# Six and ten recurrence steps in two halves' stretches instead of eight and eight, and the second attention over 66 products

## The reference, cut to what matters

```python
h = rmsnorm(x, g_pre[l]) * (1.0 + scale[:, None]) + shift[:, None]
p = h @ w_in[l]                       # (2048, 8704)
y_pool = pool_mixer(a_in, ...) * silu(a_g)
y_hgrn = hgrn2_mixer(b_q, b_f, b_i, ...) * silu(b_g)
y_conv = short_conv_mixer(c_x, c_b, c_c, conv_w[l]) * silu(c_g)
y_diff = diff_attention(d_q, d_k, d_v, ...) * silu(d_g)
# the recurrence, over chunks of tokens:
o = einsum(qc * exp(b), S) + einsum(scores, vc)
S = exp(b_last) * S + einsum(kc * exp(b_last - b), vc)
# the merge:
merged = sum(gates[n] * (y[n] @ w_merge[n]));  out = merged @ w_out[l]
x = x + gate * rmsnorm(out, g_post[l])
```

## The kernel before

| engine | offsets |
|---|---|
| SyncE | -15 `load_in3`, -13 `load_pool` (two loads, L599 and L600, counted by `a_loaded`), -1 `load_conv`, `load_gate`, +7, +13, +15 stores |
| ScalarE | -11 `pool_sigmoid` (L1078) and `sigmoids` (L1062 to L1064), -10 `affine`, -9 table preload and `logs`, -7 `key_decays`, -5 and -1 `level_decays` (L1095), 0 `query_decays` (L1101), +1 `gate_sigmoid`, `conv_sigmoid`, +5 `tokens`, +9 `squares`, +13 `root_h` (L1107, L1108) |
| VectorE | -10 `shares`, -9 `queries`, -8 `scan`, -7 to -2 differences (L1416, folded by L1421) and decays, +1, +3, +5, +7 `pick`, +11 `advance_state` (L1465, L1468), +12 `pool_out`, +14 `finish` |
| GpSimd | -4 `pool_part` (L822 to L835), 0 `decays_second`, +2 `conv_part` |
| TensorE | 0, 2, 4, 6 `rounds` (L1817), +4 `transposes`, +8 `outputs` (L1834 to L1841), +12 `norms` (L1847) |

## Time and profile before

### The profile page before, as it was taken

One profiled execution on the slowest core, in us unless ns is written; L12 is line 12 of the kernel. 1 busy time (PEld: TensorE's weight loads), 2 busy tenths in 40 slices (PEclk: granted clock), 3 DMA queues, 4 the chain that ended last, 5 costly groups with the idle time before them and its releaser, 6 DMA issues. The chain is left out here.

```text
span 2533.1 us, 35157 instructions
## 1 busy us (share of the span) xinstructions
PE 2274.4 (90%) x11572; PEld 1871.5 (74%) x11572; DVE 1434.6 (57%) x2638; ACT 1144.1 (45%) x2400; POOL 839.4 (33%) x739
## 2 busy tenths in 40 slices
PE   3698799998999889898999999999999966989898
PEld 2486677777777668687888888878888844767676
DVE  5676566655888777312766666445556334444442
ACT  3553455543544543422666666434434233434341
POOL 0113223223745645200222222124343225244353
PEclk7799999999999989999999999999999988999999
DMA  6799777757767667989464654588777676576581
GB/s 227 260 352 328 259 231 241 223 204 277 264 239 261 230 222 253 332 265 264 163 191 146 181 169 149 171 258 250 230 247 235 213 238 178 155 190 187 148 226 61
DMA packets 383963, 564.75 MB, mean 223 GB/s; under 512 B 32432, under 2 KB 248880, under 8 KB 382768
## 3 DMA queue, kind: packets, MB, share of 16 engines
q1 hardware_dynamic: 315248, 313.01, 42.0%
q10 hardware_dynamic: 68544, 249.59, 27.8%
HBM read 331.28 MB, written 231.21 MB: 222 GB/s over the span
## 5 line engine op out<-in xcount | busy, mean ns | idle before, releaser
L1682 PE MATMUL gb<-h_hi,w_both 128*128 128x512 f32 x1904 | 789.0, 414 | 87.2 <-ACT o L949 41.7
L1684 PE MATMUL gb<-h_hi,w_both 128*128 128x512 f32 x1904 | 757.7, 398 | 0.0
L1683 PE MATMUL gb<-h_lo,w_both 128*128 128x512 f32 x1904 | 756.7, 397 | 0.0
L1682 PEld LDWEIGHTS gb<-h_hi,w_both 128*128 128x128 f32 x1904 | 366.9, 193 | 171.2 <-issue 91.7
L1684 PEld LDWEIGHTS gb<-h_hi,w_both 128*128 128x128 f32 x1904 | 365.7, 192 | 81.2
L1683 PEld LDWEIGHTS gb<-h_lo,w_both 128*128 128x128 f32 x1904 | 367.7, 193 | 67.1
L949 ACT ACTIVATE o<-gb 128x512 f32<-128x512 f32 x272 | 161.4, 594 | 372.5 <-PE gb L1684 308.0
L809 POOL TENSOR_TENSOR C_prob<-C_prob,C_cf 128x512 f32<-128x512 f32 (+3 forms) x160 | 156.9, 1005 | 506.1 <-DVE C_cf L1358 492.1
L1014 ACT ACTIVATE C_prob<-C_sc,C_negm 128x512 f32<-128x512 f32 (+3 forms) x320 | 198.5, 622 | 246.6 <-DVE C_negm L1336 239.9
L1250 DVE TENSOR_TENSOR o<-gb,o 128x512 f32<-128x512 f32 x204 | 140.3, 688 | 231.0 <-PE gb L1684 220.0
L1240 DVE TENSOR_TENSOR w_both<-w,w_both 128x512 fp32r<-128x512 f32 x170 | 142.1, 836 | 171.5 <-ACT w_both L922 171.1
(11 more groups left out here) (230 smaller groups left out, 3722.6 us busy)
## 6 DMA issues: line engine op xcount, KB each, us to landing
wS_scratch<-w_both ACTq DMA_DIRECT2D x238, 512.0 KB, 4.4
w_both<-wS_scratch ACTq DMA_DIRECT2D x238, 512.0 KB, 4.3
w<-in_w_in_dram SPq DMA_DIRECT2D x68, 512.0 KB, 5.2
gT_scratch<-o SPq DMA_DIRECT2D x128, 256.0 KB, 4.6
D_gate<-gT_scratch SPq DMA_DIRECT2D x32, 1024.0 KB, 9.8
pT_scratch<-o SPq DMA_DIRECT2D x80, 256.0 KB, 4.2
C_qt<-qB_scratch SPq DMA_DIRECT2D x128, 128.0 KB, 3.4
C_ks<-kT_scratch SPq DMA_DIRECT2D x48, 256.0 KB, 5.7
```

Of the source, the lines that this page charges most:

```text
L1682: mm(to, hi[:, k, :], h_hi[j][:, k, :], start=(fresh and k == 0), stop=False, skip_group_check=True)
L1683: mm(to, hi[:, k, :], h_lo[j][:, k, :], start=False, stop=False, skip_group_check=True)
L1684: last = mm(to, lo[:, k, :], h_hi[j][:, k, :], start=False, stop=(k == KH - 1), skip_group_check=True)
```

## The change

It sets new bases: six steps in the first half's stretch, at slots 130, 146, ..., 210 (16 apart), and ten in the second's, at 367, 377, 388, 398, ..., 461 (10 and 11 in turn). Steps 6 and 7, which work on the first half's tokens, thereby run in the second half's stretch. `MIX_FROM` takes the place of `MIX_HALF` where the boundary between the stretches is meant; where the tokens' halves are meant, `MIX_HALF` stays. The second attention is spread over 66 slots, and the mixers after it start five slots earlier. eb and kt are doubled; their second copies lie in the last, unused level of QX and X. Their waits reach two steps back. `advance_state` moves from offset 11 to 10 and `pool_out` from 12 to 10.

```diff
-ATTENTION = ((50, 60), (284, 71))
-
-MIX_BASE = [130 + 12 * i for i in range(8)] + [372 + 25 * i // 2 for i in range(8)]
+ATTENTION = ((50, 60), (284, 66))
+
+MIX_BASE = [130 + 16 * i for i in range(6)] + [367 + 21 * i // 2 for i in range(10)]
+
+MIX_FROM = (0, 6, 16)
...
-            eb, qe, kt = sb("eb", [P, 2, P]), sb("qe", [P, 2, P]), sb("kt", [P, 2, P])
+            qe = sb("qe", [P, 2, P])
...
+            eb, kt = [sb("eb", [P, 2, P]), QX[:, :, NL - 1, :]], [sb("kt", [P, 2, P]), X[:, :, NL - 1, :]]
...
             def mixers_over(half):
-                n = MIX_HALF * (half + 1)
+                n = MIX_FROM[half + 1]
...
-                    if n == MIX_BASE[MIX_HALF * half] - 17:
+                    if n == MIX_BASE[MIX_FROM[half]] - 17:
                         begin_mixers(half)
...
             def key_decays(i):
                 act.wait_ge(scanned, i + 1)
-                if i:
-                    act.wait_ge(t_done, i)
+                if i >= 2:
+                    act.wait_ge(t_done, i - 1)
...
             def query_decays(i):
-                if i:
-                    act.wait_ge(state_done, i)
-                    act.wait_ge(qe_ready, i)
-                a(eb[:, :, :], b_s[:, :, :], ACT.Exp).then_inc(eb_ready, 1)
+                if i >= 2:
+                    act.wait_ge(state_done, i - 1)
+                    act.wait_ge(qe_ready, i - 1)
+                a(eb[i % 2][:, :, :], b_s[:, :, :], ACT.Exp).then_inc(eb_ready, 1)
...
-                i = mix_step(n, 11)
+                i = mix_step(n, 10)
                 if i is not None:
                     advance_state(i)
-                i = mix_step(n, 12)
+                i = mix_step(n, 10)
                 if i is not None:
                     pool_out(i)
...
                 if u >= NU:
-                    pe.wait_ge(fin_done, MIX_HALF)
-                    pe.wait_ge(yp_ready, MIX_HALF)
-                    pe.wait_ge(state_done, MIX_HALF)
+                    pe.wait_ge(fin_done, MIX_FROM[1])
+                    pe.wait_ge(yp_ready, MIX_FROM[1])
+                    pe.wait_ge(state_done, MIX_FROM[1])
...
-                if i % MIX_HALF == 0:
-                    pe.wait_ge(b_setup, i // MIX_HALF + 1)
-                    pe.wait_ge(b_consts, 16 * (9, 17)[i // MIX_HALF])
+                if i in MIX_FROM:
+                    pe.wait_ge(b_setup, MIX_FROM.index(i) + 1)
+                    pe.wait_ge(b_consts, 16 * (9, 17)[MIX_FROM.index(i)])
```

More of the change, by code:

```diff
@@ L714, in _ @@
                 for half in range(HALVES):
-                    if n == MIX_BASE[MIX_HALF * half] - 17:
+                    if n == MIX_BASE[MIX_FROM[half]] - 17:
                         begin_mixers(half)
-                    if n == MIX_BASE[MIX_HALF * half] - 16:
+                    if n == MIX_BASE[MIX_FROM[half]] - 16:
                         load_blocks(half)
@@ L1086, in key_decays @@
                 act.wait_ge(scanned, i + 1)
-                if i:
-                    act.wait_ge(t_done, i)
+                if i >= 2:
+                    act.wait_ge(t_done, i - 1)
                 for t in range(2):
-                    ins = a(kt[:, t, :], b_s[:, t, :], ACT.Exp, bias=b_s[:, t, P - 1:P], scale=-1.0)
+                    ins = a(kt[i % 2][:, t, :], b_s[:, t, :], ACT.Exp, bias=b_s[:, t, P - 1:P], scale=-1.0)
                 ins.then_inc(decayed, 1)
@@ L1424, in decay_keys @@
                 dve.wait_ge(decayed, i + 1)
-                tt(kt[:, :, :], kt[:, :, :], k_s[i % 2][:, :, :], ALU.mult).then_inc(kt_ready, 1)
+                tt(kt[i % 2][:, :, :], kt[i % 2][:, :, :], k_s[i % 2][:, :, :], ALU.mult).then_inc(kt_ready, 1)
             def decay_queries(i):
@@ L1430, in decay_queries @@
                     dve.wait_ge(o_done, i)
-                tt(qe[:, :, :], q_s[i % 2][:, :, :], eb[:, :, :], ALU.mult).then_inc(qe_ready, 1)
+                tt(qe[:, :, :], q_s[i % 2][:, :, :], eb[i % 2][:, :, :], ALU.mult).then_inc(qe_ready, 1)
             def decay_first_queries(i):
@@ L1467, in advance_state @@
                 for t in range(2):
-                    ins = stt(S[:, t, :], S[:, t, :], eb[:, t, P - 1:P], kvm[:, t, :], ALU.mult, ALU.add)
+                    ins = stt(S[:, t, :], S[:, t, :], eb[i % 2][:, t, P - 1:P], kvm[:, t, :], ALU.mult, ALU.add)
                 ins.then_inc(state_done, 1)
@@ L1855, in transposes @@
                     nc.tensor.transpose(b6[:, t, :], in3[i % 2][:, 4 + t, :], ident[:, :])
-                    last = nc.tensor.transpose(b6[:, 2 + t, :], kt[:, t, :], ident[:, :])
+                    last = nc.tensor.transpose(b6[:, 2 + t, :], kt[i % 2][:, t, :], ident[:, :])
                 last.then_inc(t_done, 1)
```

## The result

The changed kernel takes 2552.89 us (median of 7 runs, 2548.96 to 2562.11), the kernel before, on the same chip, 2536.46 us (7 runs). The ratio is 1.0081 with a 95% interval of 1.0067 to 1.0095: slower by 0.8%. Forecast were 2543 us and slower. The time lies in the range (2512 to 2567), 10 us above the forecast.

What follows compares the result with a forecast made beforehand. TensorE, busy 90% of the span, was taken as the bound. 2534.9 - 39.3 (first stretch) + 0 (attention) + 50.0 (last stretch) = 2545.6 us profiled, less 3.0 for the median: 2543 us, range 2512 to 2567.

Steps and rivals of the forecast that it cites:

- What bounds it; the prices: Whole kernel: TensorE, busy 90% of the span, is the bound; a product costs 2.72 us, a recurrence step 8.45 us.
- First stretch, -39.3 us beside the moved work: Products 130 to 229: ScalarE's queue falls apart with steps 16 apart, so 49.3 us of loss shrink to 10.
- the rest: Products 130 to 229: loss left by VectorE's full slots, 10 us for six steps, half clock included, bounds 3 and 31.
- the forecast's own test: Stated sign of being wrong: TensorE without gaps at 1.00 in the last stretch, or over 20 us lost in the first.
- Second attention, 0: Products from 284, 66 instead of 71: TensorE is the bound and released products cost the same later; 0, bounds -3 and +4.
- Last stretch, 50 us of loss: Products 367 to 475: eight late pool loads stall ScalarE, then TensorE; 33.2 us idling plus 16.8 of lower clock.
- the loop that I worked out: Last stretch: outputs free win, GpSimd's pool work, then SyncE's load; 9.6 us against 3.3 available, ScalarE standing 6.3 us.
- Lifted waits: Last stretch: doubled eb and kt lift waits at no instruction cost; the earlier state update keeps ahead of the next outputs.
- The sum: Whole kernel: 2534.9 - 39.3 + 0 + 50.0 = 2545.6 us profiled, 3.0 less for the median, say 2543 us.
- Rival 1: Last stretch: quick 2.4 us landings mostly hide the new wait, stalls too short for the clock; 2505 us, chance 0.13.
- Rival 2: Last stretch: 7.5 us landings lengthen the loop, 74.4 us lost; 2567 us; slower by over 0.5% from 5.3 us landings; chance 0.18.
- Rival 3: First stretch stays clogged by VectorE: 2.6 us stall and as much clock a step, 31 us left; 2564 us, chance 0.11.

Runs made afterwards that it cites:

- the kernel with both buffers: The changed kernel with a second win and a third s_ag copy from step 6 on; 2509.55 us, ratio 0.9904 to the kernel before.
- the third s_ag: The changed kernel with three copies of s_ag instead of two from step 6 on, win still single; 2546.12 us, ratio 1.0051 to the kernel before.

## Why the prediction was right, and where it was not

**What bounds it; the prices.** Right. 2.72 us for a product and 8.45 for a step give 378.3 us for the last stretch, and the kernel with both buffers took 378.6.

**First stretch, -39.3 us beside the moved work.** The time was forecast at about 333 us and came to 343.9; 322.7 would be without loss, so the rest is 21.2 us and not 10. Of it 14.7 is idling, 2.4 a step, at the top of my 0 to 2.5, and 6.5 is the lower clock. The mechanism was right: the queue on ScalarE has gone, none of TensorE's waits is for it any longer, and root's table loads are down to two of thirteen in the stretch. What is late next is VectorE, in slots base + 10 and + 14, as named; moving work out of the first was worth some 6 us (4 to 9.5), out of the second 4. The term that was mis-sized is the rest, by 11.2 us: I took 1.7 us a step with the clock in it, and it was 3.5. The fullest place of the changed kernel, slot 204, in order of time; product 204 starts at 891.34:

```profile
892.76 0.69 DVE L1244 TENSOR_TENSOR w_both<-s,w_both 128x512 fp32r<-128x512 f32 x1 [3.99 <-ACT w_both L926]
...
893.37 3.10 DVE L1420 TENSOR_TENSOR B_X<-B_b_s 128x128 f32<-128x128 f32 x4
...
893.53 1.30 POOL L785 TENSOR_TENSOR s<-w 128x512 f32<-128x512 f32 x1 [0.96 <-DVE w_both L1244]
...
896.50 2.12 DVE L1425 SCALAR_TENSOR_TENSOR B_X<-B_X 128x896 f32<-128x896 f32 x1
...
898.99 0.61 DVE L1472 SCALAR_TENSOR_TENSOR S<-S,B_eb,B_rs 128x128 f32<-128x128 f32 x2
...
900.04 0.68 DVE L1254 TENSOR_TENSOR o<-gb,o 128x512 f32<-128x512 f32 x1
...
900.87 0.76 PE L1686 MATMUL gb<-h_hi,w_both 128*128 128x512 f32 x1 [3.93 <-DVE o L1254]
```

The slot's work takes 7.28 us (892.76 to 900.04), inside my 6.5 to 7.9, but not by the terms that I gave. Four differences take 0.78 us each and the fold 2.12, beside GpSimd's sums of weight tiles, where I had 0.50 and 1.19: 2.0 us more. The two state updates take 0.61 where I had 1.4 to 2.8. Over the stretch the means of difference and fold were 0.46 and 1.24, as I had them; a mean hides that the long ones come together. What made the wait 3.93 us and not the 0 to 2.5 forecast is what stood beside the sum: VectorE begins the slot's work 1.42 us after the product's start, as it waits for ScalarE's half of the weight split, and the eviction behind the work takes another 0.83 to the product's start. Against the two products of cover (5.4 us) I had set the work alone. In the kernel with the state and the pool output moved out, 1.5 us of this wait went and 2.43 stayed, with the differences alone in the slot. Behind slot + 14 too there are pieces far over their usual length: at 856.65 a weight split takes 2.56 us beside a 2.12 us multiply of GpSimd, where the one at 892.76 takes 0.69. By the forecast's own test, over 20 us of loss, this step was wrong in size.

**Second attention, 0.** Right for the attention itself (1.0008 alone). The stretch to product 366 grew by 3.4 us, inside the bounds of -3 and +4, but for a reason that I had not looked for: the set-up of the mixers, which the same edit moves five slots ahead into the attention, waits on VectorE for the masks with an eviction behind it. With the set-up four slots later, the two products behind it lose nothing. The step looked at the evicting engine's share of the work and not at what the moved slots issue.

**Last stretch, 50 us of loss.** 44.5 were measured: 29.8 of idling in eight waits, the longest 4.4, against 33.2 in eight of 4.4 and 3.9; and 14.7 at the lower clock against 16.8. The number is close for reasons that are only half right. By the runs, the loop that I worked out is worth 36.4 us alone (the third s_ag). The working behind the wait holds: at one such place of that kernel (phase 6) the sigmoid starts at 1749.41 and the eviction ends at 1752.96, 3.55 us, where I had 3.61. The term that was mis-sized is the landing, 3.9 or 4.0 us in the median where I took the 5.0 of before. That is some 8 us over eight waits (25.5 of idling there, where I had 33.2), and 5.9 less at the lower clock behind them, 13.6 together. And I had left out a second wait in the same function, for the pool output of two steps back, which adds 8.1. It stands in front of the table load, so that this is no longer hidden, and in four of the eight places it came last. Two errors of opposite sign left 5.5 us; that the sum is so close is luck. (By its own terms the stall at phase 3 should have been 13.8 - 9.3 = 4.5 and not 4.4, 0.4 us in the sum.) The landings, in the changed kernel:

```profile
L604 SPq DMA_DIRECT2D B_ag_in<-pT_scratch x8: 463/471/1330, 1664.1 to 1961.7; - x8
...
DMA to landing us min/median/max: 3.7/3.9/5.1
```

**Lifted waits.** I wrote that the state update a slot earlier is ahead of the next outputs. It is, but at slot base + 10 it also came to lie beside GpSimd's long pieces, in every second step. The forecast costed it at nothing; it is a part of what the s_ag loop costs. The offset alone is not the cause, as at the old bases the update at offset 10 isn't slow. What offset 11 would do in this stretch no run shows; by the bases it would stand in the slot of the long pieces in the steps that are 11 apart.

**The sum.** 2545.6 us for the profiled execution, 2557.9 measured, 12.3 more: 11.2 of the first stretch, -5.5 of the last, 3.4 before it, and 3.2 over the parts that aren't touched (up to product 129, products 230 to 283, and the merge), where kernels with the same work differ by as much. In medians the change costs 16.4 us, and I had 10.7.

**Rivals.** Rival 1, the wait hidden, fell: TensorE's eight waits were 3.0 to 4.4 us. Its words "too short for the clock" would not have held for all stalls either. With win doubled TensorE has waits of 1.0 to 1.4 us, and behind two of them the clock was at its lower level. Such a wait, and the stretch behind it:

```profile
1784.87 0.47 PE L1692 MATMUL gb<-h_hi,w_both 128*128 128x512 f32 x1 [1.36 <-ACT o L959]
```

```profile
1785.30:1788.70 3.40, 3.40 (x10) 2.63 (x9) 2.45 (x7) 3.37 (x8) 3.32 (x2) 0.51 0.38 135
```

Rival 2, the loop longer, did not come: no landing was over 5.1 us, under its 5.3. Rival 3, VectorE in the way, had the stall right (2.6 us a step, 2.4 measured) and the clock wrong (as much again, 1.1 measured); its rest of 31 us is no further from the 21.2 measured than my 10.

**Landing and table load.** By the Trainium skill (DMA: Bandwidth & Descriptors, Anatomy of one DMA) the load would land in an estimated 2.3 us; the page gives its fit for transfers issued by GpSimd, and this one is SyncE's. The quickest took 3.7 here, so the trace again does not agree. The Trainium skill (ScalarE: Activation LUTs, What ACT_TABLE_LOAD costs) counts a drain of 1.38 us beside the table load. It does not show either: behind the table load at 1753.57, 1.28 long, the sigmoid starts at 1754.86, and in a row without a gap the last sigmoid ends at 1711.01, the table load starts at 1711.03 and the level decays at 1712.32.

## What to carry to other kernels

When periodic work moves closer together, list every buffer with its copies and ask, at the new distance, in which slot the last reader stands and in which the next writer; read all waits of the function that you have found, not the first that fits. Here two buffers of 1 KB a partition were short by one copy each, which turned -1% into +0.8%. A wait in front of an instruction on the engine that also empties TensorE's banks is paid by everything behind it; give the buffer another copy, or move the instruction, before moving the work closer. And size a full slot by the longest of its pieces beside the other engine, not by their mean over a stretch; against the cover set also how late the slot's work begins and the eviction behind it.

## What the runs showed of the hardware

A small instruction of VectorE stood still for the whole length of one of GpSimd's. The state update of 128x128 takes 348 ns where GpSimd is not in the way. With the first copy of eb it took 2177 to 2264 ns in all ten instances of the changed kernel's last stretch (duration ns min/median/max):

```profile
L1472 DVE SCALAR_TENSOR_TENSOR S<-S,B_eb,B_rs x10: 2177/2226/2264, 1663.7 to 2006.5; 128x128 f32<-128x128 f32 x10
```

That is the length of one 128x896 multiply of GpSimd (2.11 us) and little else, and the two in a row (4.38 us) end 0.15 us behind the second of the two multiplies, which ends at 1752.82. It is not the tile: with win doubled the same instruction on the same tile took 589 ns in the mean, 0.35 to 0.77 us, with GpSimd at its short pieces of 0.6 to 0.7 us. The Trainium skill (SBUF — State Buffer, Who interferes with whom) says that a VectorE instruction with two inputs in SBUF contends with a GpSimd instruction that reads SBUF, that the ports which they share are an exclusive lock, and that the order of issue decides who is blocked. The row agrees, GpSimd's multiply starting at 1748.53 and the update at 1748.59. Of the forecast this would have asked one more question: what does GpSimd issue in the slot to which the state update moves?
